# The first projection of a two-block kernel: a new order of weight blocks and of the work that leads to it

## The reference

```python
mod = jax.nn.silu(c) @ ada_w[layer] + ada_b[layer]          # 6 * 1024 wide; the same for c_ctx
mod_c = jax.nn.silu(c_ctx) @ ada_w[layer] + ada_b[layer]
sh1, sc1, g1, sh2, sc2, g2 = [m[:, None, :] for m in jnp.split(mod, 6, axis=-1)]
...
def rmsnorm(x, g):
    xf = x.astype(jnp.float32)
    y = xf * lax.rsqrt(jnp.mean(xf * xf, axis=-1, keepdims=True) + RMS_EPS)
    return y.astype(x.dtype) * g
def modulate(x, shift, scale):
    return x * (1 + scale) + shift
...
pl = xm @ w_in          # xm: normalized and modulated latent tokens
pc = cm @ w_in          # cm: the same for the context tokens
```

## Time and profile before

| what | us |
|---|---|
| median of three runs | 1913.17 |
| the profiled execution, its own time | 1912.51 |
| its span (first to last instruction) | 1910.7 |
| TensorE busy | 1741.8 (91%) |
| VectorE busy | 1123.2 (59%) |
| ScalarE busy | 983.4 (51%) |
| mean granted clock of TensorE | 0.946 |

### The profile page before, as it was taken

One profiled execution on the slowest core, in us unless ns is written; L12 is line 12 of the kernel. 1 busy time (PEld: TensorE's weight loads), 2 busy tenths in 40 slices (PEclk: granted clock), 3 DMA queues, 4 the chain that ended last, 5 costly groups with the idle time before them and its releaser, 6 DMA issues.

```text
span 1910.7 us, 27380 instructions
## 1 busy us (share of the span) xinstructions
PE 1741.8 (91%) x11008; PEld 1445.7 (76%) x11008; DVE 1123.2 (59%) x1499; ACT 983.4 (51%) x1286; POOL 71.3 (4%) x68
## 2 busy tenths in 40 slices
PE   5999989699999869999878879999959989999898
PEld 2786665588888648889656668888848988887588
DVE  2440664799989574343231278988955584634464
ACT  3322663488888544224321268888844572344352
POOL 0000000100000100000000010000010000100100
PEclk8999999799999969999989979999979998999899
DMA  8726004799999853224344469999964444264521
GB/s 333 159 88 240 26 1 187 292 398 406 409 403 402 342 228 132 88 88 144 122 176 176 154 229 411 406 408 403 401 247 147 184 149 161 60 201 159 132 67 67
DMA packets 52979, 421.73 MB, mean 221 GB/s; under 512 B 17028, under 2 KB 18180, under 8 KB 30608
## 3 DMA queue, kind: packets, MB, share of 16 engines
q1 hardware_dynamic: 26272, 364.55, 48.8%
q0 software_dynamic: 8592, 32.69, 5.5%
q10 hardware_dynamic: 18016, 23.07, 3.8%
HBM read 399.27 MB, written 21.02 MB: 220 GB/s over the span
## 4 chain that ended last, share of the span: by engine, by line
PE 82%; DVE 9%; ACT 4%; DMA 3%; issue 2%; POOL 0%; DVEq 0%; SPq 0%; ACTq 0%; POOLq 0%
PE ps L693 43%; PE ps L828 18%; PE ps L650 6%; PE ps L673 2%; PE ps L839 1%; PE ps L684 1%; PE ps L700 1%; DMA arena<-xtok_d,slot_tok 1%; DMA ring<-w_all 1%; PE ps L1226 1%; PE ps L846 1%; PE ps L1071 1%; PE ps L1042 1%; DMA hT<-h 1%; PE ps L1057 1%
## 5 line engine op out<-in xcount | busy, mean ns | idle before, releaser
L2067 DVE TENSOR_TENSOR w_lo<-ring,w_hi 128x1024 fp32r<-128x1024 f32 x384 | 452.7, 1220 | 58.9 <-ACT w_hi L1508 57.2
L1508 ACT ACTIVATE w_hi<-ring 128x1024 fp32r<-128x1024 f32 x384 | 396.4, 1057 | 101.9 <-PE ps L828 60.3
L693 PE MATMUL ps<-XT_lo,arena_r 128*128 128x256 f32 (+1 forms) x1712 | 387.3, 301 | 9.9 <-DVE ring_r L1937 7.2
L693 PEld LDWEIGHTS ps<-XT_lo,arena_r 128*128 128x128 f32 x1712 | 283.3, 191 | 25.7 <-issue 7.9
L828 PE MATMUL ps<-w_hi,x_hi 128*128 128x256 f32 (+1 forms) x768 | 250.1, 326 | 4.9 <-issue 4.8
L828 PE MATMUL ps<-w_lo,x_hi 128*128 128x256 f32 (+1 forms) x768 | 245.8, 320 | 0.0
L828 PE MATMUL ps<-w_hi,x_lo 128*128 128x256 f32 (+1 forms) x768 | 245.8, 320 | 0.0
L693 PE MATMUL ps<-arena_r 128*128 128x512 f32 (+1 forms) x624 | 226.4, 363 | 13.6 <-DVE ring_r L2289 7.5
L1937 DVE TENSOR_TENSOR ring_r<-ring,arena_r 128x1024 fp32r<-128x1024 f32 x96 | 113.7, 1223 | 123.2 <-ACT arena_r L1419 123.0
L693 PE MATMUL ps<-XT_lo,ring_r 128*128 128x256 f32 x640 | 180.5, 282 | 0.0
L828 PEld LDWEIGHTS ps<-w_hi,x_hi 128*128 128x128 f32 x768 | 146.9, 191 | 21.6 <-issue 6.2
(11 more groups left out here) (334 smaller groups left out, 2573.1 us busy)
## 6 DMA issues: line engine op xcount, KB each, us to landing
ring<-w_all SPq DMA_DIRECT2D x172, 2048.0 KB, 9.1
y_d<-arena ACTq DMA_DIRECT2D x32, 512.0 KB, 10.1
arena<-toep_d POOLq DMA_DIRECT2D x16, 384.0 KB, 10.3
arena<-rpb ACTq DMA_DIRECT2D x16, 192.0 KB, 6.1
xtok_d<-arena ACTq DMA_DIRECT2D x6, 512.0 KB, 2.7
hT<-h SPq DMA_DIRECT2D x1, 2048.0 KB, 12.9
arena<-cb_d POOLq DMA_DIRECT2D x1, 1536.0 KB, 8.8
arena<-cc_d POOLq DMA_DIRECT2D x1, 959.0 KB, 5.4
```

Source lines behind the costliest of these rows:

```text
L693: last = nc.tensor.matmul(out, a, b, start=(first and i == 0), stop=(final and i == 2))
L1508: nc.scalar.activation(w_hi[:, q], slot(b, "p (q c) -> p q c", q=4)[:, q], ACT.Copy).then_inc(hi_rdy, 1)
L2067: nc.vector.tensor_tensor(w_lo[:, q], slot(base + n, "p (q c) -> p q c", q=4)[:, q], as_f32(w_hi[:, q]), ALU.subtract).then_inc(*split_sig ...
```

## The change

- The list of blocks becomes: modulation 0, 2, 1 (one of shift, one of scale, one of shift), first block of the projection, modulation 3, then the other four of the projection (`MOD_ORDER`, `MIX_AT`). The fourth to load is therefore a block of the projection, in slot 0; modulation 3 is in slot 1.
- Modulation 0 is taken to columns before the sum of squares. Seven of the eight squares are added on VectorE (`norm_partial`, which other norms of the kernel have already), and TensorE sums two rows only (`norm_part`).
- `gains` are made in halves: rows 0 to 3 after modulation 0 and 2, rows 4 to 7 after modulation 1 and 3. mod_ready counts one more from here on, and the waits for it elsewhere are raised by one; GpSimd's load of ca now waits for 2.
- VectorE scales rows 0 to 3, goes on to XT_lo of those rows with the splits of units 0 to 3 between them, and scales rows 4 to 7 only then. ScalarE has the same splits between its rows of mix_x.
- TensorE works on units 0 to 3 together, row k by row k, into four banks; rows of modulation 3 stand behind k = 1, its columns behind k = 2. The slot of the first block is released when all four are done.
- The three small operations on final_g move behind the split of unit 4.

```diff
@@ -51,11 +51,15 @@
-ADA_CUTS = (0, 4, 8, 13, 16, 24)
+ADA_CUTS = (0, 3, 4, 8, 13, 16, 24)
 ADA_BLOCKS = [range(a, b) for a, b in zip(ADA_CUTS, ADA_CUTS[1:])]
 B_ADA0 = 0
-B_MIX = B_ADA0 + 4
-B_ADA1 = B_MIX + 5
+B_MIX0 = B_ADA0 + 3
+B_ADA3RD = B_MIX0 + 1
+B_MIX1 = B_ADA3RD + 1
+MIX_AT = (B_MIX0, *range(B_MIX1, B_MIX1 + 4))
+MOD_ORDER = (0, 2, 1, 3)
+B_ADA1 = B_MIX1 + 4
 B_MIXO = B_ADA1 + 4
...
@@ -616,7 +620,7 @@
-            pool.wait_ge(mod_ready, 1)
+            pool.wait_ge(mod_ready, 2)
             pool.dma_start(ca, ca_d).then_inc(ld_ca, 16)
...
@@ -711,7 +715,7 @@
                 a, b = NORM_COLS[i]
-                pe.wait_ge(nm_part, (i + 1) // 2)
+                pe.wait_ge(nm_part, (1, 2, 0, 3)[i])
                 nc.tensor.matmul(ps[:, 7, 0:b - a], ones, squares_of(i)[:, 0], start=True, stop=False)
...
@@ -974,24 +978,34 @@
             pe.wait_ge(tick_ready, 1)
             pe.sem_inc(split_used, 3)
-            mod_rows_of(0, 0)
+            mod_rows_of(0, 4)
             pe.wait_ge(ld_cst, 16)
+            mod_cols_of(0, 6)
+            norm_part(0)
+            for a in (1, 2):
+                mod_rows_of(a, 4 + a % 2)
+                mod_cols_of(a, (2, 6)[a - 1], after=a)
             for k in range(KT):
-                norm_sum(0, k)
-            for a in range(1, 4):
-                mod_rows_of(a, a % 2)
-                mod_cols_of(a - 1, 2)
-            mod_cols_of(3, 2)
-            unit = 0
-            for b in range(5):
+                pe.wait_ge(nm_lo, k + 1)
+                for unit in range(4):
+                    if k == 0:
+                        pe.wait_ge(dw_lo, unit + 1)
+                    last = three_terms(ps[:, unit, :], mix_hi(unit)[:, k], mix_part(unit, ring_r)[:, k], mix_x[:, k], XT_lo[:, k],
+                                       k == 0, k == KT - 1)
+                    if k == KT - 1:
+                        last.then_inc(mx_mm, 1)
+                if k == 1:
+                    mod_rows_of(3, 5)
+                if k == 2:
+                    mod_cols_of(3, 7, after=3)
+            release(MIX_AT[0])
+            unit = 4
+            for b in range(1, 5):
                 for m in range((4, 4, 4, 2, 0)[b]):
-                    if unit >= 4:
-                        pe.wait_ge(mx_ev, unit - 3)
+                    pe.wait_ge(mx_ev, unit - 3)
                     pe.wait_ge(dw_lo, unit + 1)
                     w, w2 = mix_hi(unit), mix_part(unit, ring_r)
                     for k in range(KT):
-                        if unit == 0:
-                            pe.wait_ge(nm_lo, k + 1)
                         last = three_terms(ps[:, unit % 4, :], w[:, k], w2[:, k], mix_x[:, k], XT_lo[:, k], k == 0, k == KT - 1)
                     last.then_inc(mx_mm, 1)
...
@@ -1008,7 +1022,7 @@
                         unit += 1
-                release(B_MIX + b)
+                release(MIX_AT[b])
             pe.wait_ge(mx_ev, unit)
...
@@ -1445,7 +1459,7 @@
                 a, b = NORM_COLS[i]
-                act.wait_ge(mod_ready, i + 1)
+                act.wait_ge(mod_ready, i + 2)
                 for n, k in enumerate(ROUTER_K[i // 2]):
...
@@ -1591,30 +1605,35 @@
             def mix_split(p):
-                n = B_MIX + p // 4
+                n = MIX_AT[p // 4]
                 if p % 4 == 0:
                     act.wait_ge(w_full[n % SLOTS], 16 * (n // SLOTS + 1))
...
                 nc.scalar.activation(mix_hi(p), mix_part(p, ring), ACT.Copy).then_inc(dw_hi, 1)
+            rows_out(0, 4)
+            table(ACT.Sqrt)
             act.wait_ge(ld_h, 16)
             for k in range(KT):
                 norm_square(0, k)
             norm_root(0)
-            for a in range(4):
-                rows_out(a, a % 2)
-            mix_split(0)
-            act.wait_ge(mod_ready, 1)
+            rows_out(1, 5)
+            rows_out(2, 4)
             for k in range(KT):
+                act.wait_ge(mod_ready, 1 + k // 4)
                 act.wait_ge(nm_tmp, k + 1)
                 for seg in range(2):
...
                                                 bias=modc[:, 0, k, seg:seg + 1])
                 last.then_inc(nm_x, 1)
-            for p in range(1, 5):
-                mix_split(p)
+                if 1 <= k < 4:
+                    mix_split(k - 1)
+                if k == 3:
+                    mix_split(3)
+                    rows_out(3, 5)
+            mix_split(4)
             for r in range(ROWS):
                 for kr in range(ROWS):
...
@@ -1898,11 +1917,19 @@
                 dve.wait_ge(mt_mm, 12 if a == 10 else a + 1)
-                layer, m = a // 12, 4 * (a % 12)
+                layer, m = a // 12, 4 * (MOD_ORDER[a] if a < 4 else a % 12)
                 nc.vector.tensor_tensor(modc[:, layer, m:m + 4], ps[:, bank, at:at + 8].rearrange("p (m s) -> p m s", s=2),
...
                                         ALU.add).then_inc(mt_ev, 1)
-                if a % 6 == 3:
+                if a in (1, 3):
+
+                    dve.wait_ge(mt_ev, a + 1)
+                    half_k = slice(m - 8, m - 4)
+                    nc.vector.scalar_tensor_tensor(
+                        gains[:, 0, half_k], modc[:, 0, m:m + 4], 1.0,
+                        sm[:, SM["norm_g"]][:, half_k].unsqueeze(2).broadcast_to([P, 4, 2]), ALU.add, ALU.mult
+                    ).then_inc(mod_ready, 1)
+                elif a % 6 == 3:
...
@@ -2183,22 +2210,34 @@
             dve.wait_ge(ld_cst, 16)
             nc.vector.tensor_copy(tok_bf[:, :], cst[:, CST["tok"]])
+            mods_out(0, 6)
+            for m in range(KT):
+                norm_partial(0, m)
+            dve.wait_ge(nm_std, 1)
+            link(nc.vector.reciprocal(inv_rms[:, 0:T], inv_rms[:, 0:T]))
             dve.wait_ge(ld_h, 16)
-            norm(0)
-            for a in range(4):
-                mods_out(a, 2)
+
+            def scaled(k):
+
+                nc.vector.tensor_tensor(XT[:, k], hT[:, k], inv_rms[:, 0:T], ALU.mult).then_inc(nm_tmp, 1)
+
+            for k in range(4):
+                scaled(k)
+            mods_out(1, 2)
             def mix_split(p):
...
                 nc.vector.tensor_tensor(mix_part(p, ring_r), mix_part(p, ring), as_f32(mix_hi(p)), ALU.subtract).then_inc(dw_lo, 1)
-            mix_split(0)
-            dve.wait_ge(mod_ready, 1)
-            link(nc.vector.tensor_tensor(sum_w, final_g, final_g, ALU.mult))
-            nc.vector.tensor_scalar(sum_w, sum_w, EPS, None, ALU.add)
-            link(nc.vector.tensor_tensor(final_w, final_w, final_g, ALU.mult))
             for k in range(KT):
+                if k == 4:
+                    mix_split(3)
+                    for late in range(4, KT):
+                        scaled(late)
+                    mods_out(2, 6, 8)
+                    mods_out(3, 7, 16)
+                dve.wait_ge(mod_ready, 1 + k // 4)
                 dve.wait_ge(nm_x, k + 1)
                 for seg in range(2):
...
@@ -2206,7 +2245,13 @@
                 link(last)
                 nc.vector.tensor_tensor(XT_lo[:, k], XT[:, k], as_f32(mix_x[:, k]), ALU.subtract).then_inc(nm_lo, 1)
-            for p in range(1, 12):
+                if 1 <= k < 4:
+                    mix_split(k - 1)
+            mix_split(4)
+            link(nc.vector.tensor_tensor(sum_w, final_g, final_g, ALU.mult))
+            nc.vector.tensor_scalar(sum_w, sum_w, EPS, None, ALU.add)
+            link(nc.vector.tensor_tensor(final_w, final_w, final_g, ALU.mult))
+            for p in range(5, 12):
                 mix_split(p)
...
@@ -2631,8 +2676,10 @@
     ada = np.concatenate([weight_blocks(a["ada_w"][layer], D, 512) for layer in range(2)])
+    ada = ada[[*MOD_ORDER, *range(4, 24)]]
     ada = [ada[r.start:r.stop] for r in ADA_BLOCKS]
-    blocks = [ada[0], weight_blocks(a["mixab_w_in"][0], D, 512), ada[1], weight_blocks(a["mixab_w_out"][0], D, 512), ada[2]]
+    mix = weight_blocks(a["mixab_w_in"][0], D, 512)
+    blocks = [ada[0], mix[:1], ada[1], mix[1:], ada[2], weight_blocks(a["mixab_w_out"][0], D, 512), ada[3]]
```

More of the change, by code:

```diff
@@ L246, in block_of @@
             cut = max(c for c in ADA_CUTS if c <= a)
-            return dict(zip(ADA_CUTS, (B_ADA0, B_ADA1, B_ADA2, B_ADA3, B_ADA4)))[cut] + a - cut
+            return dict(zip(ADA_CUTS, (B_ADA0, B_ADA3RD, B_ADA1, B_ADA2, B_ADA3, B_ADA4)))[cut] + a - cut
         fnT = area(0, 1024).rearrange("p (f t) -> p f t", f=2)
@@ L1930, in norm @@
                         mods_out(9, 6)
-                        dve.wait_ge(mod_ready, 2)
+                        dve.wait_ge(mod_ready, 3)
             def z_split(*ps_):
@@ L2643 @@
     blocks.append(expert_blocks(0))
-    blocks.append(ada[3])
+    blocks.append(ada[4])
     rw = a["ret_w_in"][0]
@@ L2649 @@
     blocks.append(weight_blocks(rw[:, 2048:], D, 512))
-    blocks.append(ada[4])
+    blocks.append(ada[5])
     blocks.append(weight_blocks(a["ret_w_out"][0], 2048, 256))
```

## The result

| | before | after |
|---|---|---|
| median of six runs each | 1911.84 | 1919.9 (1915.45 to 1923.87) |
| ratio after / before | | 1.0044, 95% interval 1.0033 to 1.0056 |
| span of the profiled execution | 1910.7 | 1921.7 |
| its own time | 1912.51 | 1923.87 |
| TensorE busy | 1741.8 | 1735.8 |

The kernel is slower by 0.44%, 8.1 us in the medians, and its median is the forecast 1920. The profiled execution is the longest of the six; the next lines are from it, and they show more of the loss than the median does.

The account below looks back on a forecast made before the run. TensorE bounds the kernel, so time moves with unit 4's start (74.66 us before). ScalarE's rpb issues delay it to 79.7: +5.0, plus +1.9 for clock, gives 1919.4 for the profiled execution, forecast 1920; likeliest range 1917 to 1923, eight in ten 1911.5 to 1926.

Parts of the forecast that it names:

- second scales: Second half of the scales, which mix_x of rows 4 to 7 waits for: ready at 56.0 us.
- first rpb issue: ScalarE's sixteen rpb load issues wait behind mix_x of rows 4 to 7: begin at 56.0 us, not 47.97.
- unit 3 done: TensorE finishes the first four units at 69.6 us; the release lets SyncE issue two weight blocks.
- Adds and sum: Norm at the start: six VectorE adds from 16.3 to 20.8 us, then TensorE's four passes end at 24.2.
- Start of mix_x: ScalarE's mix_x starts at 33.0 us, the middle between full clock (before 31.4) and half clock (34.6); before, 43.88.
- The collision: Open rpb issues meet two weight blocks from about 71.1 us: issues end at 78.5 to 79, bounds 74.7 and 82.3.
- far-end rival: Rpb stands still while two weight blocks flow: issues end at 84 us, unit 4 at 85, total 1925; chance 0.12.
- My price by that rule: If engines take turns between queues at every packet, rpb keeps a share and its issues end near 82 us.
- The clock: TensorE restarts at unit 4 after some ten idle microseconds: 3.5 us at half clock lose 1.8 to 1.9 us.
- The sum: Late start of unit 4 +5.0 and clock +1.9 make +6.9 us on the profiled execution, 1919.4.
- Nothing behind unit 4 changes: Claim that everything after unit 4's start stays as before, including weights, mask and later loads.
- Rows 9: Trace of the kernel before, 49.5 to 51 us: weight queue moved 25 packets, rpb none; read as weights going first.

Follow-up runs that it names:

- e3_hold: Changed kernel with SyncE holding its two weight blocks behind unit 3 until all rpb loads have landed; ratio 0.9988 to the kernel before.
- e10_before_padded: Kernel before plus twelve two-column matmuls at the head of TensorE's stream; ratio 0.9978 to the kernel before.
- e1_late: Changed kernel with the sixteen rpb loads issued four at a time behind the splits after ScalarE's copies of units 4 to 7; ratio 0.9949 to the kernel before.
- e4_halves: Changed kernel with eight of the sixteen rpb loads issued earlier, in ScalarE's idle stretch; ratio 0.9941 to the kernel before.
- e8_before_delayed: Kernel before with one added wait, so that ScalarE issues no rpb load until unit 1 is finished; ratio 1.0079 to the kernel before.
- e9_padded: Changed kernel with eight rpb loads early, last modulation rows ahead of the units and twelve two-column matmuls at TensorE's head; ratio 0.9959 to the kernel before.
- e7_rows_ahead: Changed kernel with eight rpb loads in ScalarE's idle stretch and the last modulation rows ahead of the units; ratio 0.9926 to the kernel before.

## Why the prediction was right, and where it was not

The sign, the place and the mechanism held: second scales 54.5 (56.0 forecast), first rpb issue 54.88 (56.0), unit 3 done 68.5 (69.6), SyncE's two blocks issued at 68.73, with three rpb issues open when their packets began to flow near 71 (3.2 forecast), TensorE idle until ScalarE's first copy right behind the last issue, then half clock for some 5 us (3.5 forecast). What each term became:

- **Adds and sum.** Six adds from 16.32 to 20.64 (16.3 to 20.8) and TensorE's sum until 24.5 (24.2): right.
- **Start of mix_x.** 31.45, forecast 33.0 between 31.4 and 34.6. The rows of block 1 at 24.48 took 2.83 us, the columns 1.05 and the rows of block 2 1.90: the clock rose soon behind the norm, and the early end of the bounds would have been right. All up to the first row of k is 1.6 us early (four splits at 42.7 instead of 44.3), which is still seen at the second scales.
- **The collision.** This is the term that was mis-sized. I gave the open issues some 7.6 us (71.1 to 78.5 or 79) as the middle between 1.11 and 3.5 us each. They took 10.05 + 3.45 + 0.96 = 14.5 us, and issuing ended at 85.4. The upper bound, 3.5 each, was read from issues with a short stretch of weights in their way; one issue lasted 10.05 us while two whole blocks flowed. The far-end rival, unit 4 at 85, was the better account of this execution (86.12). Its reason was half right: rpb does not stand still behind the weights, it gets a packet in turn, but one of 1/60 the size. The Trainium skill (DMA: Bandwidth & Descriptors, "Queues, rings and completion order") says that an engine turns to the next queue at every packet. The counts of 214 and 195 agree, if what the trace counts is such a packet. No run shows that it is; the same section of the Trainium skill puts several descriptors into one packet. My price by that rule, an end near 82, was too mild (85.4), because I took a turn for a share. Without the weights the issues end at 75.4 in e3_hold, where the forecast had 74.7.
- **The clock.** 24.77 - 22.39 = 2.4 us lost in the first group (1.9 forecast).
- **The sum.** In the profiled execution unit 4 is 11.5 us late instead of 5.0, +13.8 with the clock (111.00 - 97.16), and at the end of the span +11.0: 2.8 are given back behind it. The sum said +6.9.
- **"Nothing behind unit 4 changes."** This failed. Behind 1434 us, where nothing is edited, the changed kernel takes 473.8 us against 476.4, so 2.6 us come back. 1.6 of them have come by the reciprocal near 1647 us and 1.4 between those near 1747 and 1835; some tenths are lost again at the end. The first part may be the missing pause, but that is an inference: e10_before_padded gains 3.1 us there, and the changed kernel was not run padded. For the second part no cause is known: e1_late and e3_hold, with the same order on TensorE as the changed kernel, gain nothing and 2.7 us there.

Rows 9, which I set against turns between the queues, are no evidence against them. The first rpb packet passes only between 52 and 53 us, more than 4 us behind the first issue at 47.97, so before that rpb may have had nothing to take a turn with. DMA queues of the kernel before, 48 to 52 us (q0: ca), with no row of q10:

```profile
q1 hardware_dynamic: 74, 1.21, 71.9%
q0 software_dynamic: 74, 0.42, 26.2%
```

So 1920 is met partly by luck. In the traced execution a collision priced too low and a gift in the tail that no step named leave +11.0 us where the sum said +6.9; it is the median, 4 us below that execution, that meets the forecast (its 8.1 us over the kernel before have an interval of 6.3 to 10.7, by the ratio). How the six runs spread over 8.4 us (1915.45 to 1923.87) is open: a collision shorter than the 14.5 us of the trace in the other five would do it, but only one of them was traced. That the issues are the gate is shown by e1_late, e4_halves and e8_before_delayed; that the collision makes some 10 us of the wait, by the traces of e3_hold and of the changed kernel.

## What to carry to other kernels

A DMA issue is an instruction in its engine's order: what stands behind it waits until the queue takes it, and this can be ten microseconds when its packets are small and another queue streams large ones. Before moving work earlier, list the issues that stand between the engine's last early job and its first late one, and move them into a stretch where that engine idles (here worth 1.0%: 0.9941 / 1.0044). And a difference of a few microseconds far behind an edit need not come from what was edited: a handful of harmless instructions at the head switched 5.5 to 5.8 us here, and kernels with one and the same order on TensorE still differed by 3 us in that stretch. So one trace each does not price an edit to the microsecond.

## What was not expected of the hardware

- Two queues with work share by packets, not by bytes: 214 packets of some 15 KB beside 195 of 256 bytes in 8 us.
- The first packet of the rpb loads passed more than 4 us behind their first issue in the kernel before, with two other queues busy. Why so late is open.
- A pause of 0.50 to 1.09 us in TensorE's stream came and went with twelve tiny matmuls at its head, and with it 5.5 to 5.8 us up to the end. The granted clock of 0.72 to 0.74 in the six us behind it is one part; a second lies near 1800 us, where the clock also differs between kernels without the pause. What exactly TensorE waits for in it is open: one packet of the instruction queue passes some 2 us ahead of it in before and e9_padded, but in e7_rows_ahead and e10_before_padded as well.
- e9_padded loses another 3.8 us to e7_rows_ahead between 352 and 687 us (0.1 behind at the start of the first product of the experts there, 3.84 at the reciprocal of the norm at 687.34) and 1.8 more up to the reciprocal at 1424.78, though it differs only in the twelve matmuls. The mean clock of 600 to 687 us is 0.84 against 0.88. This is not shown to be position: between the reciprocals at 337.65 and 697.51 us of the kernel before, the changed kernel, e1_late, e3_hold and e4_halves, with the same order on TensorE, take from 358.4 to 361.9 us, as wide a spread as between e7_rows_ahead (357.5) and e9_padded (361.4). The medians of e9_padded and e7_rows_ahead, each against the kernel before on its own chip, are 0.33% apart, some 6 us, where the two traces are 11.1 us apart.
